# A hybrid encoder block in fp32: VectorE's substitution put ahead of the second masked product, and ScalarE's copies placed anew around the blocks' round trip

## The reference

```python
def step(S, inp):
    rt, wt, kt, vt, kkt, at = inp
    sa = jnp.einsum('bhvk,bhk->bhv', S, -kkt)
    S = S * wt[:, :, None, :] + sa[..., None] * (kkt * at)[:, :, None, :] + vt[..., None] * kt[:, :, None, :]
    return S, jnp.einsum('bhvk,bhk->bhv', S, rt)
```

```python
s = jnp.einsum('bhcqd,bhckd->bhcqk', qi, kh).astype(jnp.float32) * scale
pr = jax.nn.softmax(s, axis=-1)
attn = pr[:, :, 0] - lam * pr[:, :, 1]
```

## Time and profile before

| | us |
|---|---|
| median of 3 runs | 1256.37 |
| lowest and highest | 1255.52, 1256.54 |
| the profiled execution | 1255.78 |
| its span in the trace | 1254.0 |
| TensorE busy | 1202.1 |
| VectorE, ScalarE busy | 310.6, 197.2 |
| moved by DMA | 445.52 MB |

### The profile page before, as it was taken

The page is one execution under the profiler, slowest core; times in us unless marked ns, Lnnn a source line. Parts: engine busy times, 40 slices in busy tenths (PEclk is TensorE's granted clock), DMA queues, the critical chain, the costliest instruction groups (busy, mean ns, idle before and its releaser), DMA issues.

```text
span 1254.0 us, 17482 instructions
## 1 busy us (share of the span) xinstructions
PE 1202.1 (96%) x7452; PEld 576.0 (46%) x7452; DVE 310.6 (25%) x771; ACT 197.2 (16%) x371; POOL 14.2 (1%) x56
## 2 busy tenths in 40 slices
PE   7997999999999999999999999998999999999997
PEld 6786888888833333333333333332333333333333
DVE  5755235113321112112112211111111211111212
ACT  2322243002211111111111111111111111111101
POOL 4000000000000000000000000000000000000000
PEclk9998999999999999999999999999999999999999
DMA  9332213855889999999999999999999999999995
GB/s 324 137 112 77 73 66 115 371 219 212 337 326 428 421 415 434 429 430 428 434 432 434 432 427 433 434 433 432 432 429 434 432 434 432 430 431 433 426 427 228
DMA packets 29922, 445.52 MB, mean 355 GB/s; under 512 B 8432, under 2 KB 8816, under 8 KB 11440
## 3 DMA queue, kind: packets, MB, share of 16 engines
q1 hardware_dynamic: 24944, 443.74, 84.3%
q10 hardware_dynamic: 4928, 1.05, 0.4%
HBM read 443.47 MB, written 1.31 MB: 355 GB/s over the span
## 4 chain that ended last, share of the span: by engine, by line
PE 70%; DMA 25%; ACT 2%; DVE 1%; issue 1%; ACTq 0%; SPq 0%; DVEq 0%
PE ps L1519 21%; DMA ring<-in_moe_w 15%; PE ps L1559 14%; PE ps L960 10%; DMA arena<-in_moe_w 9%; PE ps L981 7%; PE ps L1463 4%; PE ps L1437 3%; PE ps L1422 2%; PE ps L1451 1%; ACT arena L908 1%; PE ps L1168 1%; PE ps L1456 1%; PE ps L995 1%; DMA ring<-in_w_in 1%
## 5 line engine op out<-in xcount | busy, mean ns | idle before, releaser
L1519 PE MATMUL ps<-ring,arena 128*64 128x512 f32 x1248 | 273.6, 593 | 13.8 <-DMA ring<-in_moe_w 13.2
L1519 PE MATMUL ps<-arena 128*64 128x512 f32 x792 | 174.0, 593 | 8.4 <-DMA arena<-in_moe_w 8.2
L1519 PEld LDWEIGHTS ps<-ring,arena 128*64 128x64 f32 x1248 | 88.9, 137 | 194.2 <-issue 173.2
L1559 PE MATMUL ps<-ring,arena 128*64 128x512 f32 x576 | 127.7, 595 | 0.0
L900 ACT ACTIVATE arena<-arena 128x512 f32<-128x512 f32 x31 | 19.5, 630 | 678.8 <-DVE arena L2119 678.8
L2119 DVE TENSOR_SCALAR arena<-ps 128x512 f32<-128x512 f32 x31 | 21.4, 691 | 397.2 <-PE ps L1519 397.2
L960 PE MATMUL ps<-arena,ring 128*128 128x256 f32 x480 | 107.5, 384 | 8.2 <-DVE arena L1691 7.3
L1519 PEld LDWEIGHTS ps<-arena 128*64 128x64 f32 x792 | 56.4, 137 | 123.3 <-issue 109.6
L960 PEld LDWEIGHTS ps<-arena,ring 128*128 128x128 f32 x480 | 91.5, 192 | 21.7 <-issue 8.0
L1559 PE MATMUL ps<-arena 128*64 128x512 f32 x408 | 90.7, 595 | 0.8 <-DMA arena<-in_moe_w 0.8
L2132 DVE COPY arena<-ps 128x512 f32<-128x512 f32 x32 | 22.1, 692 | 235.2 <-PE ps L1559 235.2
(11 more groups left out here) (308 smaller groups left out, 872.5 us busy)
## 6 DMA issues: line engine op xcount, KB each, us to landing
ring<-in_moe_w SPq DMA_DIRECT2D x51, 4096.0 KB, 35.2
arena<-in_moe_w SPq DMA_DIRECT2D x32, 4096.0 KB, 36.6
arena<-in_moe_w SPq DMA_DIRECT2D x12, 2048.0 KB, 27.5
ring<-in_moe_w SPq DMA_DIRECT2D x11, 2048.0 KB, 32.8
ring<-in_w_in SPq DMA_DIRECT2D x12, 1024.0 KB, 5.2
ring<-in_wkv_x SPq DMA_DIRECT2D x8, 1024.0 KB, 4.8
ring<-in_w_out SPq DMA_DIRECT2D x4, 1024.0 KB, 4.7
ring<-in_wq_x SPq DMA_DIRECT2D x4, 1024.0 KB, 7.2
```

The costliest lines, as they stand in the source:

```text
L1519: ins = t.matmul(ps[c * BLK:(c + 1) * BLK, 4 + b, :], xeT[:, col:col + BLK], w(k % 4)[:, f0:f0 + 512], start=False, stop=(k == KC - 1), sk ...
L1559: ins = t.matmul(ps[c * BLK:(c + 1) * BLK, 7, :], src[:, col:col + BLK], w(k // 2)[:, f0:f0 + 512], start=(k == 0), stop=(k == KC - 1), sk ...
```

## The change

On VectorE the substitution now stands directly behind `masked(0)`, and `masked(1)` behind the substitution. On ScalarE `natural_rows(1)` moves from ahead of the round trip to behind it, and the copy of `in10` moves from behind the eight reads to between the write of the solved blocks and the wait for it. On TensorE `in10` is computed ahead of the transposes of `turn_natural(1)`, which until now stood ahead of it. No instruction is added or taken away.

```diff
             natural_rows(0)
             copy(kd[:, 0:2, :], "in9", two)
-            natural_rows(1)
 
             act.wait_ge(sem("X16_ready"), 1)
             act.wait_ge(sem("const_ready"), 1)
             act.dma_start(blocks[1].rearrange("j q a b -> (j q) a b"), X16[:, :, :]).then_inc(sem("X_blocks_out"), 16)
+            copy(kd[:, 2:4, :], "in10", two)
             act.wait_ge(sem("X_blocks_out"), 16)
             for j in range(P // SUB):
                 cols = slice(SUB * j % CH, SUB * j % CH + SUB)
                 act.dma_start(XTb[SUB * j:SUB * j + SUB, :, :, cols].rearrange("c i h a -> c (i h) a"),
                               blocks[1, j].rearrange("q c a -> c q a")).then_inc(sem("XT_in"), 16)
-            copy(kd[:, 2:4, :], "in10", two)
+            natural_rows(1)
...
             chunk_products(1)
+            turned("in10", xT)
             turn_natural(1)
-            turned("in10", xT)
...
             masked(0)
-            masked(1)
...
             dve.sem_inc(sem("X16_ready"), 1)
+            masked(1)
```

## The result

| | before | after |
|---|---|---|
| median of 4 runs each, us | 1256.45 | 1247.42 |
| lowest and highest | 1255.52, 1257.95 | 1247.03, 1248.22 |
| span of the profiled execution | 1254.0 | 1245.4 |
| mean granted clock | 0.993 | 0.999 |

The ratio is 0.9927 with a 95% interval of 0.9914 to 0.994: 9.0 us or 0.7% faster. The prediction said 1252.3 with a range down to 1249.0. The sign was right; the gain is more than twice what was forecast (4.1 us) and the time lies outside the range. On another chip the same changed kernel came to a ratio of 0.9937 (0.9921 to 0.9953), 7.7 us.

What follows compares the result with a forecast made beforehand. The prediction took ScalarE's stream as the path to the scores, with everything later hanging on TensorE. It summed -6.7 (reads start) + 0.5 (two copies for one) + 2.05 (held issues) = -4.1 us: 1252.3, range 1249.0 to 1254.0.

Steps and rivals of the forecast that it cites:

- The substitution: VectorE: starts at 88.4 once the blocks are read back and ends at 96.75, 7.5 us earlier.
- TensorE's order: TensorE: `in10` starts behind the chunk products and ends at 101.79 instead of 103.62; `bo` ends near 106.1.
- The write was covered: ScalarE: the solved blocks' write, out at 96.8, lands by 101.6, covered by the copy of `in10` by at least 0.8 us.
- The end follows: Behind the scores: their shift reaches the end whole, with the first expert load at 220.1 instead of 224.22.
- the third rival: Experts' stream: the gain is lost at the end and the time stays at 1256.4; chance 0.10.
- the issues under a load: ScalarE's eight reads behind the load of `kv0`: held issues take 5.88 us instead of 3.82, costing 2.05.
- The second row on which the term stood: Packets at the blocks' write, issued 0.63 us behind a load: only SP's moved up to 107.4, then ScalarE's.
- the first rival: ScalarE's reads: no hold at the queue, scores at 107.8, time 1250.2, or 1249.2 with the clock kept; chance 0.24.
- The reads' start: ScalarE: the eight reads start behind the copy of `in10`, at 102.46 instead of 109.14, 6.7 us earlier.
- Copy to scores: From ScalarE's copies of `natural_rows(1)` to TensorE's scores: 0.35 us.
- The clock: TensorE, idle 3.7 us before the scores: clock falls to half again, term 0; if it stays up, 1.0 us more won.

Runs made afterwards that it cites:

- the first variant: Changed kernel with ScalarE's two copies of `natural_rows(1)` moved ahead of the eight reads; 1245.91 us, ratio 0.9914.
- the two variants: Changed kernel with `natural_rows(1)` ahead of the reads, 1245.91 us; the second also puts scores ahead of `bo` and VectorE's reading of `bo` behind the maxima, 1246.96 us.
- e1: Kernel before with VectorE's part of the change alone, `masked(1)` behind the substitution; 1248.42 us, ratio 0.9944.
- e3: Changed kernel with TensorE's old order, the transposes of `turn_natural(1)` ahead of `in10` again; 1255.84 us, ratio 0.9992.

## Why the prediction was wrong in size

**The substitution** held: predicted end 96.75, write at 96.8; the write went out at 96.96. **TensorE's order** held: `in10` predicted to end at 101.79, ended at 101.9, and `bo` ended at 106.04 for a predicted 106.1. **The write was covered**: it landed 2.7 us behind its issue, not 4.84, and the load ahead of it, issued some 3.5 us earlier, moved its last packets between 97 and 98. **The end follows**: of 7.51 us at `z1`, 7.27 reach the first expert load, and the span is 8.6 us shorter, so the third rival is refuted.

**The failed step is the issues under a load**, the term of +2.05 us. Measured were 4.16 us for the eight instead of 5.88, so +0.34. I read line 745 wrongly. Its sum of 5.88 us under a load and 3.82 without one looked like the price of the load, but 1.2 us of it is one long issue at 80.4, when the load was over: the packets of that very stretch, above, were there to be read before. The second row on which the term stood was read rightly, but does not carry the term: the packets of the blocks' write came after the load's, and so did 96% of the reads' packets after the change. What failed is the step from there to the issues, that "the fourth is held until packets move". In the first variant five reads were issued without one of their packets moving, and the longest issue of all eight was 801 ns. A load delays the landings, which had cover enough here, and hardly the issuing, on which the scores wait. In the changed kernel the reads were issued 0.02 us behind the load, in the two variants 0.88 and 0.89, and in those no small packet moved in the first 3 us; so the small size or the direction of the reads is not what let 87 of them through. Whether the 0.02 us is, no run separates further. Of the rivals the first, with 0.24, named the case that came true, and of its two reasons the second held, that line 745 stalled late, when little was moving; that reads are taken in more readily than writes is not shown.

**The reads' start** was put behind the end of the copy of `in10` (102.46). They started with it, at 101.94: 0.52 us. The first variant shows it again: its first read is issued at 102.87, ahead of the start (102.97) of the last of the three copies that stand in front of it. Nothing in the rows of before showed a DMA's issue that stood directly behind a copy, and I took the copy's end by assumption.

**Copy to scores** took 0.14 us for a predicted 0.35. With 0.03 us between the last issue and the copies the three steps make up the 2.48 us by which the scores came earlier than 109.85: 1.72 (issues) + 0.52 + 0.21 + 0.03.

**The clock** was a step that held for its input, and the input was wrong. With 3.66, 4.24, 4.92, 6.72 and 6.84 us of idle time before the scores they ran at half clock for all or part of their time (2.08, 2.08, 1.66, 2.08, 2.08 us); at 1.34 to 1.64, in six executions, they did not (1.16). In between the rows don't agree: behind 1.97 us of idle time `in10` kept the full clock in e1 (7.07 us), behind 1.98 it lost it in e3 (8.76). Since the idle time followed from the held issues, the error in that term came back a second time: 0.92 us.

Together: 6.60 at the scores, 0.92 for their clock, 0.24 lost, against 7.27 us measured at the first expert load. By the edited stretch that is what the change is worth, and it gives 1249.1, just inside the range. The profiled pair shows 8.6 and the first medians 9.0; the other chip shows 7.7. The surplus in the pair is the router's clock, 0.99, and the last load, 0.35; how much of the medians' surplus is the change's own stays open, as said above. The prediction did not look at that stage: its half clock was in the trace of before, and a sentence on it would have said that about 1 us can come or go there. The range ended at 1249.0 because I gave the first rival 1249.2 as its best value and allowed nothing for such spread.

## What to carry to other kernels

An instruction that waits for another engine and stands ahead of a long chain that doesn't need it makes the whole chain wait with it; look for it on the engine where the chain begins, since here that one move alone gave 7.35 of 7.61 us. When a row is taken as the price of contention, look at what moved in exactly the stretch of its longest member before the row is used as a term. Packets that wait and issues that wait are two things; read each from its own rows. And when several engines' orders are changed together, cost each with the others' old order: here the moves on ScalarE and TensorE added only 0.26 us to the substitution, and ScalarE's without TensorE's put the reads behind a late copy, so that the gain was gone.

## What the runs showed of the hardware

- Eight small reads issued 0.02 us behind a load of 1 MB got 87 of their 2176 packets through while it was in full flow; issued 0.88 us behind it, none in 3 us. In the first case landings went from 1.8 to 2.1 us up to 3.6 to 5.4, while issuing them took only 0.34 us more in all.
- ScalarE issued a DMA while the copy ahead of it still ran: at 101.94, with a copy from 101.93 to 102.53.
- An issue of ScalarE took 1.99 us with no load on the DMA engines, beside one packet of the instruction queue. That the packet is the cause is not shown.
- Two executions of the same kernel differed by 10 us, in stretches outside the edits. The 40 products that start near 11.7 us took 8.9 us in seven of the 14 profiled executions and 10.6 to 11.3 in the other seven, at a granted clock that the rows give as full in both, and everything behind them moves by it; and in the router's stage the clock fell in 4 of 14 executions, at a price of 0.9 to 4.5 us. The rest, 3.5 us, lies behind line 1519 and was not traced. A comparison of single profiled executions of this kernel has to be made stretch by stretch.
